# Gathering the expert inputs of a two-block transformer once, sorted by expert, and cutting each expert's columns out with GpSimd

## What is computed

```python
def hierarchical_moe(hn, w_router_group, w_router_expert, w_gate, w_up, w_down):
    g_probs = softmax(t @ w_router_group);  g_w, g_idx = top_k(g_probs, 1)
    # the two best of the 8 experts of that group
    top_l, top_i = top_k(e_in_group, 2)
    weights = softmax(top_l) * g_w
    comb = sum(one_hot(ids, 32) * weights[..., None], axis=1)
    for e in range(32):
        hid = silu(t @ w_gate[e]) * (t @ w_up[e])          # 2048 -> 256
        out = out + (hid @ w_down[e]) * comb[:, e:e + 1]   # 256 -> 2048
```

## Time and profile before

| | |
|---|---|
| device time, 3 runs | 2243.16, 2243.33, 2245.48 us, median 2243.33 |
| the profiled execution, first to last instruction | 2242.7 us |
| what lies around that span, to the median | 0.6 us |
| PE busy | 2203.2 us, 98% of the span |
| DVE, ACT, POOL busy | 59%, 41%, 1% |
| DMA over the span | mean 231 GB/s |

### The profile page before, as it was taken

The page is one execution under the profiler, slowest core; times in us unless marked ns, Lnnn a source line. Parts: engine busy times, 40 slices in busy tenths (PEclk is TensorE's granted clock), DMA queues, the critical chain, the costliest instruction groups (busy, mean ns, idle before and its releaser), DMA issues.

```text
span 2242.7 us, 32809 instructions
## 1 busy us (share of the span) xinstructions
PE 2203.2 (98%) x12483; PEld 1750.0 (78%) x12483; DVE 1316.9 (59%) x1768; ACT 916.9 (41%) x1272; POOL 15.7 (1%) x30
## 2 busy tenths in 40 slices
PE   9999999999999998999999999999999999999998
PEld 8886888666656664788888878888888888888886
DVE  7797566322222223666666755767777777764453
ACT  5564454422222221554445444554434343433342
POOL 1000000000000000000000000000000000000000
PEclk9999999999999999999999999999999999999999
DMA  7764465699999999557655556546666666666664
GB/s 254 215 195 132 136 179 184 272 417 419 418 419 420 420 417 411 146 171 224 212 172 160 162 161 185 169 150 188 189 188 189 189 189 189 187 207 195 194 193 131
DMA packets 283044, 518.45 MB, mean 231 GB/s; under 512 B 22016, under 2 KB 194096, under 8 KB 257968
## 3 DMA queue, kind: packets, MB, share of 16 engines
q1 hardware_dynamic: 280128, 505.50, 66.2%
q0 software_dynamic: 2800, 11.34, 1.5%
HBM read 514.63 MB, written 5.27 MB: 232 GB/s over the span
## 4 chain that ended last, share of the span: by engine, by line
PE 91%; DVE 4%; ACT 2%; DMA 1%; issue 1%; DVEq 0%; SPq 0%; ACTq 0%
PE acc L670 30%; PE acc L691 24%; PE acc L694 12%; PE ps L1112 10%; PE acc L1134 5%; PE tp L1062 2%; DVE wlo L1900 1%; PE tp L779 1%; PE tp L1074 1%; PE ps L847 1%; PE ps L1062 1%; DMA mw<-in_w_expert_down 1%; DMA mw<-in_w_expert_gate 1%; PE tp L1075 1%; PE ps L1074 1%
## 5 line engine op out<-in xcount | busy, mean ns | idle before, releaser
L1900 DVE TENSOR_TENSOR wlo<-raw,whi 128x1024 fp32r<-128x1024 f32 x572 | 675.9, 1221 | 207.2 <-ACT whi L1399 202.8
L691 PE MATMUL acc<-xhl,whi 128*128 128x512 f32 x2496 | 790.6, 398 | 1.6 <-DVE wlo L1900 0.7
L1399 ACT ACTIVATE whi<-raw 128x1024 fp32r<-128x1024 f32 x572 | 582.5, 1054 | 355.9 <-DMA raw<-in_w_down 128.4
L694 PEld LDWEIGHTS acc<-xhl,wlo 128*128 128x128 f32 x2496 | 468.9, 188 | 110.7
L694 PE MATMUL acc<-xhl,wlo 128*128 128x256 f32 x2496 | 490.9, 278 | 0.0
L691 PEld LDWEIGHTS acc<-xhl,whi 128*128 128x128 f32 x2496 | 381.6, 189 | 5.8 <-issue 3.0
L1112 PE MATMUL ps<-mw,xg 128*64 128x256 f32 x2048 | 231.1, 381 | 3.0 <-DMA mw<-in_w_expert_gate 1.6
L1112 PEld LDWEIGHTS ps<-mw,xg 128*64 128x64 f32 x2048 | 145.2, 137 | 89.5 <-issue 20.7
L670 PE MATMUL acc<-whi,xhl 128*128 128x512 f32 x480 | 157.2, 397 | 0.0
L670 PE MATMUL acc<-whi,ah 128*128 128x512 f32 x336 | 130.7, 389 | 0.0
L670 PE MATMUL acc<-wlo,ah 128*128 128x512 f32 x336 | 130.7, 389 | 0.0
(11 more groups left out here) (431 smaller groups left out, 2462.2 us busy)
## 6 DMA issues: line engine op xcount, KB each, us to landing
raw<-in_w_in SPq DMA_DIRECT2D x352, 256.0 KB, 3.0
raw<-in_w_up SPq DMA_DIRECT2D x352, 256.0 KB, 2.9
mw<-in_w_expert_gate SPq DMA_DIRECT2D x64, 1024.0 KB, 10.9
mw<-in_w_expert_up SPq DMA_DIRECT2D x64, 1024.0 KB, 8.6
mw<-in_w_expert_down SPq DMA_DIRECT2D x64, 1024.0 KB, 11.6
raw<-in_w_down SPq DMA_DIRECT2D x176, 256.0 KB, 3.3
raw<-in_w_out SPq DMA_DIRECT2D x128, 256.0 KB, 3.1
raw<-in_w_ple_gate SPq DMA_DIRECT2D x64, 256.0 KB, 3.2
```

Of the source, the lines that this page charges most:

```text
L691: pe.matmul(out(ct).rearrange("p (m n) -> p m n", m=2), wh[:, ct * P:ct * P + P], ahl[:, :, k, :], start=first, stop=False, skip_group_che ...
L694: mm = pe.matmul(out(ct)[:, S:2 * S], wl[:, ct * P:ct * P + P], ahl[:, 0, k, :], start=False, stop=last, skip_group_check=True)
L1399: act.activation(whi[:, m % RING, :], raw[:, m % RING, :], ACT.Copy).then_inc(hi_ready, 1)
L1900: dve.tensor_tensor(wlo[:, m % RING, :], raw[:, m % RING, :], whi[:, m % RING, :], ALU.subtract).then_inc(lo_ready, 1)
```

## The change

All 512 assigned rows are gathered in one go, into 512 columns sorted by expert, instead of 2048 columns with 64 for each expert. DVE works out where each expert's columns start (`start_e`, a running sum of the counts), the column of each row (`packed`), and a matrix of ones and zeros of 512 columns (`g_pack`). PE gathers with 4 matmuls of 512 columns per block of 128 features (L1100), 16 blocks: 8 before the first `gate_up`, 8 between `gate_up(0, 0)` and `gate_up(0, 1)`. ACT copies them into `xp`. GpSimd then reads each expert's start into a register and copies the 64 columns from there into the buffer that PE uses for the pair (`xg_first` for pair 0, in two halves of 8 blocks; two buffers in turn for the others). PE waits for these copies (`x_copied`). A window of 64 columns can hold rows of the next expert too; the slots matrix `G`, which brings results back, is made against the window's start. `h` is written to memory (2 MB, SP) for the branch of the overfull experts.

```diff
+            def copies(g, ks):
+                for e in range(2):
+                    first = pool.value_load(window_i[0:1, 2 * g + e:2 * g + e + 1], min_val=0, max_val=LAST_START)
+                    pool.tensor_copy(xg[g][:, ks, e * SLOTS:(e + 1) * SLOTS],
+                                     xp[:, ks, bass.ds(first, SLOTS)]).then_inc(x_copied, 1)
+            pool.wait_ge(packed_ready, 1)
+            for half in range(2):
+                for b in range(3):
+                    pool.wait_ge(t_read[b], read_times(b, 8 * (half + 1)))
+                copies(0, slice(8 * half, 8 * half + 8))
+            for g in range(1, PAIRS):
+                if g >= 3:
+                    pool.wait_ge(w_used, STEPS * (g - 2) + 4)
+                copies(g, slice(0, KT))
...
             for g in range(PAIRS):
                 for c in range(4):
+                    if g == 0 and c == 2:
+                        sp.wait_ge(acc_free[0], MIX_END[0])
+                        sp.wait_ge(acc_free[1], MIX_END[1])
+                        sp.dma_start(h_d, h[:, :, :]).then_inc(h_out, 16)
                     load_step(STEPS * g + c, ...)
...
-            def gather(q, k):
-                if k == 0:
-                    pe.wait_ge(quad_ready, q + 1)
+            def gather(kt):
+                if kt % 8 == 0:
+                    pe.wait_ge(xl_ready, TT * (kt // 8 + 1))
                 o = use()
-                for j in range(2):
-                    for m in range(2 * TT):
-                        mm = pe.matmul(o[:, j * 2 * P:(j + 1) * 2 * P], x_k[m // TT][:, m % TT, 2 * k + j, :], g_quad[:, q % 2, m % TT, :], ...)
+                for m in range(2 * TT):
+                    mm = pe.matmul(o[:, :], x_k[m // TT][:, m % TT, kt, :], g_pack[:, m % TT, :], ...)
...
+                if g == 0 and c < 2:
+                    pe.wait_ge(x_copied, 2 * c + 2)
                 pe.wait_ge(w_in_g[step % STEP], w_landed(step))
...
-            pe.wait_ge(xl_ready, TT)
-            for k in range(8):
-                gather(0, k)
-            pe.wait_ge(slots_ready, 2)
+            pe.wait_ge(packed_ready, 1)
+            for kt in range(8):
+                gather(kt)
             def move(g, q):
                 if g:
                     scatter(g - 1, 2 * q)
-                if g < PAIRS - 2:
-                    gather(g // 2 + 1, g % 2 * 4 + q)
-                if g:
                     scatter(g - 1, 2 * q + 1)
             for g in range(PAIRS):
                 gate_up(g, 0)
+                if g == 0:
+                    for kt in range(8, KT):
+                        gather(kt)
                 gate_up(g, 1)
...
+            own(dve.tensor_copy(count_e[:, :], ps[0][:, 64:96]))
+            own(dve.tensor_tensor_scan(until_e[:, :], window[:, :], count_e[:, :], 0.0, ALU.mult, ALU.add))
+            own(dve.tensor_tensor(start_e[:, :], until_e[:, :], count_e[:, :], ALU.subtract))
+            own(dve.tensor_tensor(place[:, :, :], rank, start_e[:, :].unsqueeze(1).to_broadcast(each), ALU.add))
...
+                    own(dve.tensor_tensor_reduce(pos[:, t, :], place[:, t, :], one_hot[:, t, :], 1.0, 0.0, ALU.mult, ALU.add,
+                                                 packed[:, j, t:t + 1]))
...
+                own(dve.tensor_scalar(g_pack[:, t, :], iota_pack[:, :], packed[:, 0, t:t + 1], None, ALU.is_equal))
+                own(dve.scalar_tensor_tensor(g_pack[:, t, :], iota_pack[:, :], packed[:, 1, t:t + 1], g_pack[:, t, :], ...))
+            dve.sem_inc(packed_ready, 1)
+            low_rows(1)
```

More of the change, by code:

```diff
@@ L1644, in _ @@
             act.wait_ge(n_inv, rows.n)
[L1645 to L1648, removed]
+            for half in range(2):
+                ks = slice(8 * half, 8 * half + 8)
+                for t in range(TT):
+                    act.activation(x_hi[:, t, ks, :], h[:, t, :].rearrange("p (q k) -> p k q", k=KT)[:, ks, :], ACT.Copy,
+                                   scale=rstd2[:, 1, t:t + 1]).then_inc(xh_ready, 1)
+                embedded(half)
             act.wait_ge(rt_read, 2)
@@ L1737, in _ @@
                 after_steps(act)
+                act.wait_ge(ov_h, 16)
+                for t in range(TT):
+                    act.activation(h_was[:, t, :], h_was[:, t, :], ACT.Copy, scale=rstd2[:, 1, t:t + 1]).then_inc(ov_x, 1)
                 for k in range(KT // 2):
@@ L2342, in _ @@
             own(dve.tensor_copy(tri_b[:, :], tri[:, :]))
+            own(dve.tensor_scalar(firsts[:, :], iota[:, 0:PACK // SLOTS], float(SLOTS), None, ALU.mult))
+            mine()
+            like = [P, PACK // SLOTS, SLOTS]
+            own(dve.tensor_tensor(iota_pack[:, :].rearrange("p (a s) -> p a s", s=SLOTS), iota[:, :].unsqueeze(1).to_broadcast(like),
+                                  firsts[:, :].unsqueeze(2).to_broadcast(like), ALU.add))
             dve.wait_ge(n_inv, rows.n)
@@ L2387, in _, with low_rows @@
             dve.sem_inc(taken_ready, 1)
-            def slot_columns(first, end):
+            def low_rows(half):
+                ks = slice(8 * half, 8 * half + 8)
                 for t in range(TT):
-                    like = [P, end - first, SLOTS]
-                    own(dve.tensor_tensor(G[:, t, first * SLOTS:end * SLOTS].rearrange("p (e s) -> p e s", s=SLOTS),
-                                          pos[:, t, first:end].unsqueeze(2).to_broadcast(like),
-                                          iota[:, :].unsqueeze(1).to_broadcast(like), ALU.is_equal))
@@ L2403, in _ @@
             low_rows(0)
+            each = [P, TT, N_EXPERTS]
             dve.wait_ge(rank_mm, 1)
             rank = ps[0][:, 0:64].rearrange("p (t e) -> p t e", t=TT)
-            own(dve.scalar_tensor_tensor(pos[:, :, :], rank, 1.0, taken[:, :, :], ALU.add, ALU.mult))
+            own(dve.tensor_copy(count_e[:, :], ps[0][:, 64:96]))
+            own(dve.memset(window[:, :], 1.0))
+            mine()
+            own(dve.tensor_tensor_scan(until_e[:, :], window[:, :], count_e[:, :], 0.0, ALU.mult, ALU.add))
@@ new lines, in _ @@
+            for t in range(TT):
+                own(dve.tensor_scalar(g_pack[:, t, :], iota_pack[:, :], packed[:, 0, t:t + 1], None, ALU.is_equal))
+            mine()
+            for t in range(TT):
+                own(dve.scalar_tensor_tensor(g_pack[:, t, :], iota_pack[:, :], packed[:, 1, t:t + 1], g_pack[:, t, :],
+                                             ALU.is_equal, ALU.add))
+            mine()
+            dve.sem_inc(packed_ready, 1)
+            low_rows(1)
+            own(dve.tensor_tensor(place[:, :, :], place[:, :, :], window[:, :].unsqueeze(1).to_broadcast(each), ALU.subtract))
@@ L2407, in _ @@
+            mine()
+            own(dve.scalar_tensor_tensor(pos[:, :, :], place[:, :, :], 1.0, taken[:, :, :], ALU.add, ALU.mult))
             mine()
@@ L2439, in _ @@
             own(dve.tensor_tensor(c3[:, 2, :, :], c_rest[:, :, :], c3[:, 1, :, :], ALU.subtract))
-            slot_columns(8, N_EXPERTS)
+            for t in range(TT):
+                like = [P, N_EXPERTS, SLOTS]
+                own(dve.tensor_tensor(G[:, t, :].rearrange("p (e s) -> p e s", s=SLOTS), pos[:, t, :].unsqueeze(2).to_broadcast(like),
+                                      iota[:, :].unsqueeze(1).to_broadcast(like), ALU.is_equal))
             mine()
```

130 lines of the change are left out of this document (66 added, 64 removed).

## The result

The changed kernel takes 2253.9 us (median of 4 runs, 2252.03 to 2254.94), the kernel before 2244.08 on the same chip (4 runs, 2243.16 to 2245.48). The ratio is 1.0045, with a 95% interval of 1.0033 to 1.0057: slower by 9.8 us, where 2256.0 and slower had been forecast.

A forecast was written before the change was run, and what follows sets the result against it. The weight transfers at 419 GB/s were taken to bound the expert stage. The head's terms put T at 440.4 against a break-even of 427.7, 12.7 us later; 2242.7 + 12.7 = 2255.4, forecast 2256, range 2247.5 to 2264.

The forecast's parts named there:

- T: Moment the second `gate_up` of pair 0 is done and step 5 is issued; 423.05 us before, 440.4 forecast.
- T + 461.0: End of the expert stage: with the queue full from step 5 on, it ends 461.0 us after that step's issue.
- It stays full, and nothing is added here: Queue after T: step 8 issued by T + 16, steps 5 to 7 keeping it busy until T + 5.5 + 15.
- The 5.5 us for latency and filling: Expert stage: time beyond 440.4 us of transfers between step 8's issue and the last step's start, kept for the forecast.
- The first rival: Expert stage: the queue takes more than 419 GB/s; without any limit 40 us faster, 2203; chance 0.06.
- break-even: Value of T at which the change neither gains nor loses: 888.69 - 461.0 = 427.7 us.
- The clock losses: Head of the stage: 1.7 us each in the first eight blocks and the two `gate_up` steps of pair 0.
- The waits: TensorE waiting for GpSimd ahead of each `gate_up` of pair 0: two copies and two register reads, 3.1 us each.
- a sign of being wrong: GpSimd's copies taking under 0.5 us or over 2 us each would show the prediction wrong.
- The start: Start of TensorE's gather after VectorE's chain: about 404.8 us, bounds 403.8 to 405.8, against 405.40 before.
- the copy of `h`: Write of 2.1 MB to memory behind the first two steps, 5 us at 419 GB/s, claimed hidden.
- the 46 us themselves: TensorE's gather work removed after pair 0 starts, 46 us, counted as nothing since the transfers cover it.

The follow-up runs named there:

- experiment 1: The changed kernel with all 16 blocks gathered ahead of the first `gate_up`; 2243.42 us, ratio 0.9993 to the kernel before.
- experiment 3: The changed kernel with 18 unread matmuls of 512 columns filling TensorE's wait for GpSimd's first copies; 2249.01 us, ratio 1.0023 to the kernel before.
- experiment 4: Half the bytes in every weight transfer from step 4 on, on both kernels: 2203.99 us for the changed kernel, 2238.31 for the kernel before.
- experiment 5: The changed kernel with 14 unread matmuls ahead of the first `down` of pairs 1 to 13; 2255.85 us, ratio 1.005 to the kernel before.
- experiment 6: The changed kernel without the copy of `h` to memory and its waits; 2254.83 us, ratio 1.0051 to the kernel before.
- experiment 2: The changed kernel with VectorE's `G` writes held until GpSimd's first pair of copies is done; 2250.94 us, ratio 1.0027 to the kernel before.
- experiment 7: The changed kernel with the gather in two parts of 256 columns and `G` writes after pair 0's copies; 2243.42 us, ratio 0.9998 to the kernel before.

## Why the prediction was right

**What bounds the stage: right, from three sides.** The rest of the kernel follows the last dry spot of the queue. T + 461.0 was the rule; measured are T + 461.4 in the changed kernel (436.5 to 897.95), T + 461.0 in experiment 1 and T + 459.8 in experiment 3.

In the changed kernel the rule came out by two misses that nearly cancel. "It stays full, and nothing is added here" was wrong: steps 5 to 7 had landed by about T + 16.5 and not T + 20.5, step 8 came at T + 17, one later than the bound, and the queue dipped from 452 to 456 us. At 229 in place of 420 GB/s that is some 1.8 us of its time, an estimate. The 5.5 us for latency and filling, taken from the kernel before, were too many on the other side: experiment 3, in which the queue stayed full, needed 4.3.

Halving the bytes uncovers 34.3 us, giving work back costs some 2. The first rival, a queue that takes more once TensorE asks, is gone: TensorE asks in nearly every step, waiting up to 2.6 us at some, and gets 420 GB/s. Its price was right all the same: with the limit off, the rival's sum gave 2203, and experiment 4 took 2204. The 435 GB/s of "DMA: Bandwidth & Descriptors" in the Trainium skill, Specifications, which would have made the kernel 4 us faster than before, was not reached over the stage in any run here: it took 420 GB/s in the changed kernel and in experiment 5.

**The size of T's delay: 12.7 us predicted, 8.8 measured against the same break-even** (436.5 less 427.7; with the 0.4 by which the rule was short, the last `down` is 9.3 us later). The sum's terms, in us, with what the changed kernel's profile shows and what the three profiles with the same head show (experiments 4, 5 and 6):

| term | predicted | changed kernel | same head |
|---|---|---|---|
| gather starts at | 404.8 | 403.4 | 404.4 to 404.5 |
| first eight blocks | 9.3 | 7.6 | 7.6 |
| their end to the last copy by ACT | 0.9 | 0.7 | 0.7 |
| first wait for GpSimd | 3.1 | 4.4 | 4.4 to 4.5 |
| `gate_up(0, 0)` | 5.3 | 6.4 | 5.2 |
| second eight blocks and ACT | 8.6 | 8.3 | 8.2 |
| second wait for GpSimd | 3.1 | 2.1 | 2.1 |
| `gate_up(0, 1)` | 5.3 | 3.7 | 5.4 |
| T | 440.4 | 436.5 | 437.9 to 438.2 |

The terms that are off are about the clock, GpSimd and the start. *The clock losses:* 1.7 us was taken three times, by analogy with a 3.24 us gap. The gap ahead of the gathers shrank to 1.63 us (1.60 to 1.64 in the other profiles) and cost nothing: that 1.7 was too much in every profile. Behind the two waits the profiles differ: one fall of 2.7 and none in the changed kernel, falls of 1.5 and 1.7 in the three others, where 3.4 had been summed. So the price for these two was about right, and it is the changed kernel's profile that came out 0.7 us cheaper. *The waits:* a copy of 512 elements takes 0.61 to 0.63 us, nearer to the slope of the memset rows (0.53) than to their scaled whole (0.97). A register read with its small operations takes some 0.5 us against 0.6 (0.29 and 0.15 for the two longest in the rows below, 0.8 in all for the first), and the sum counted two reads in each wait where one counts: the second ran beneath the first copy, and the second copy began 0.05 us behind the first. So the second wait was a third shorter than predicted. The first was longer, because the `G` write held GpSimd up, the cost that the prediction cited for it without a price; of the 34 copies, this one alone took over 2 us, which the prediction had named as a sign of being wrong. The two misses nearly cancel, and that is luck. *The start:* 0.7 us of the 1.4 lie in a router that ended earlier (the first `x_lo` starts at 395.27 and not 396.00), the rest in VectorE's chain (4.2 us from the count to the end of `g_pack` in place of 4.9).

**Hidden as claimed:** the copy of `h` (experiment 6), and the 46 us themselves.

What stays open: which waits of about 3 us let the clock fall. In six profiles TensorE waits 2.79 or 2.80 us at the same place; the 96 matmuls behind it take 10.58 us, at full clock, in two (the changed kernel and experiment 3), 12.27 in three (4, 5 and 6), and 13.53 in one (2). What tells them apart is not shown. Also, TensorE's first gather started between 403.4 us (the changed kernel, the earliest) and 404.6 (experiments 1 and 7) in profiles of the same head; of the 1.2 us between the changed kernel and experiment 1, all stand already at the start of `x_lo` (395.27 against 396.46), behind the router.

## What to carry to other kernels

Where both an engine and the DMA queues show full, ask what each does where the other has less to do: one lighter pair at the end of the stage told that the queue would not yield, and so that 46 us of removed work would bring nothing and a head 9 us later would cost 9. In a stage that runs at the queue's rate, count forward from the last place where the queue is dry, and check that the steps behind it are issued in time, since one more dip moves that place; time saved behind it is worth nothing, and time added ahead of it is paid in full. When a new engine is put into that head, look for work that can stand over its latency: the same change with its gathers in one piece (experiment 1) costs nothing, since each copy then lies under TensorE's next work.

## What the hardware showed that was not expected

GpSimd's second copy, 413.50 to 416.08 us, took 2.58 us in place of 0.61 to 0.63. It began under the second of VectorE's two `G` writes, which read two inputs from SBUF, and ended 0.5 us behind it (415.6). Moving the writes behind the copies took the 2 us away (experiment 2). Only the second copy suffered: the first one, at 0.63 us, had begun 0.1 us ahead of the same write and ended 0.5 us into it. In the five other profiles with the write over these copies, two copies took 3.23 to 3.33 us. VectorE's second write by itself:

```profile
412.90 2.70 DVE L2488 TENSOR_TENSOR G<-pos,iota 128x2048 bf16<-128x2048 f32 x1
```

The Trainium skill, "GPSIMD Engine Reference", section 8, names this contention; the size is this case's.

After 5.15 us of waiting TensorE ran at a granted clock of 0.50, 1.2 GHz, which made a 3.67 us step 6.39 us (5.20 to 5.24 in the three other profiles with this wait); kept busy with unread matmuls it did not fall (experiment 3). A copy of 1024 elements per partition on GpSimd took 1.05 us, 0.84 ns for each element beyond 512. GpSimd's register reads and copies, with the shortest, median and longest in ns:

```profile
L608 POOLq TENSOR_LOAD <-window_i x34: 283/287/500, 411.9 to 833.0; - x34
L608 POOLq FUSED_REGOPS  x34: 152/152/188, 412.4 to 833.3; - x34
L609 POOL COPY xg_turn<-xp x30: 1040/1052/1062, 432.8 to 834.0; 128x1024 f32 x30
L609 POOL COPY xg_first<-xp x4: 613/622/2577, 412.8 to 432.2; 128x512 f32 x4
```
